# Token mixer of a 256-token block: gates as tanh, selection in two parts, norms ahead of splits

## The chip, the cores and the metric

The kernel is one program on one core of a Trainium2 chip. The metric is device time in microseconds (us) from launch to end, median of three runs. TensorE (PE) multiplies, ScalarE (ACT) and VectorE (DVE) work on rows of 128 partitions, GpSimd (POOL) and SyncE (SP) here issue the transfers from HBM.

## The reference, cut to what matters

Two transformer blocks follow each other on 256 tokens of width 1024. The change is in the token mixer of the second one:

```python
(qa, ka, va, qb, kb, vb, qi, ki, wi, xc, yc, gates) = split(xn @ w_in)
y_a = moba_attention(qa, ka, va, bias)                  # 8 heads, here plain causal
y_b = dsa_attention(qb, kb, vb, qi, ki, wi, bias)       # 8 heads, keys: the 64 best of
#   score = sum_h wi[h] * relu(qi[h] . ki), per query; others get -1e30
y_c = rg_lru(causal_depthwise_conv(xc, conv_w, conv_b), ...) * gelu(yc)
#   r, i = sigmoid(block matmuls); log_a = -8 r softplus(-lam); a = exp(log_a)
#   u = sqrt(1 - a*a) * i * x;  h[t] = a[t] h[t-1] + u[t]
g = sigmoid(gates).reshape(B, S, 3, 1024)
merged = g[:,:,0] * (y_a @ w_pa) + g[:,:,1] * (y_b @ w_pb) + g[:,:,2] * (y_c @ w_pc)
x = x + merged @ w_o
```

All is fp32. Each product is made from three matmuls: every operand is split into a high part (rounded to the matmul's input type) and a low part (the rest), and high x high, high x low and low x high are summed in PSUM.

## The kernel before, in words

Weights stream through four slots ("units" 0 to 3). For each step SP loads the four units of `raw`; ACT makes the high part `wh` (L1521), DVE the low part `wl` = `raw` - `wh` (L2243), and PE multiplies (L569 to L571). A unit of `wh` and `wl` is written again as soon as PE has used it, so that the two splits run one step ahead of PE: while PE is in a step, the units of the next are split one by one behind it. SP loads a unit again as soon as DVE has made its low part (`lo_done`).

The mixer's steps are, in order: qa, ka, va, xc, qi, kw, yc, qb, kb, vb, then g0 to g5 (the gates, 512 columns each), then pa, pb, pc (`step_down` and `rows_by_tile` on the three branches), then two halves of `w_o`. A gate step is 48 matmuls of 512 columns, 12 per unit. PSUM has two halves of four banks that the steps take in turn. When a step's sums are complete, ACT copies them out (`read_gate` L2031, `read_values`, `read_half`), DVE copies its share and tells PE that the half is free by a small memset on `emptied` (`close` L2276, `take_step` L3015). Side work of the attention uses the other half in the middle of a step: PE yields after each unit, waits for `emptied` of the step before (`other_emptied` L1290) and runs, for group n of four heads (n = 0, 1: branch a; 2, 3: branch b), `attend_scores(n)` (L1330), later `turn_probabilities(n)` (L1340 to L1342) and `attend_values(n)` (L1362). Between them DVE adds the bias (`biased(n)` L2948, L2950), and the maxima (`maxima(n)` L2962 to L2967, which for branch b also adds the selection's mask), ACT takes the exponents and their sums (`softmax(n)` L2045), DVE scales by the sums (`normalise(n)` L2974 to L2976), and both copy the turned probabilities out (`take_turned(n)` L2051 and L2981). `choose` (L2928) finds the 64 best by four rounds of `pick`, twice: a round is a maximum and a replacement of eight values for each of two tiles; the mask is written at the end. `convolve` (L3003) is the depthwise convolution, 12 instructions; its result is needed by the recurrent gates (`recurrent_gates` L1312, in step g3) and, since it shares memory with them, by gates g2 to g5.

The order of the work on each engine is written out by hand: ACT's list is the run of calls from L2080 on, DVE's from L3025 on, where `parts(u)` is the split of unit u. An engine's queue is strictly in order. PE's points are the ones in L1364 to L1490. After g5, DVE runs the recurrence (`tensor_tensor_scan` L3128), the product with gelu (L3131, `yc_ready`), low part (`yc_lo` L3134); ACT makes its high part (L2175); then DVE multiplies the gates into pa and pb (`gate_rows` L3141), adds, multiplies pc's tiles (`gate_tile` L3146), and adds them (`merge_tile` L3153, `merged`). PE turns the merged tiles (`turn_merged`, matmul line L1467), ACT and DVE make high and low parts (L2074, L3159), and the two `w_o` steps run on them.

ACT's functions live in tables; the compiler puts an `ACT_TABLE_LOAD` ahead of a function that is not in the table that is loaded.

Of the kernel before, what the change touches and what calls it, by code (L numbers as in the profile page):

```python
# [183 lines left out]
def build(nc, a, out):  # L184
    ctx = ExitStack()
    with ctx:
# [369 lines left out]
        def _(pe):  # L556
# [929 lines left out]
            for t, j in rows_by_tile(half, ctx_h, ctx_l, 0, True, False, wo_rows):  # L1486
                if (t, j) == (0, 1):
                    turn_merged(1, 4 - half)
                elif (t, j) == (0, 3):
                    pe.wait_ge(mg_lo, 2)  # L1490
# [14 lines left out]
        def _(act):  # L1505
# [525 lines left out]
            def read_gate(c):  # L2031

                hb = step_full()
                if c == 2:
                    act.wait_ge(xcv_ready, 1)
                T.mark(act.activation(gates3[c // 2][:, :, c % 2, :], ps[:, hb:hb + 2, :], ACT.Sigmoid), act_evac)
# [34 lines left out]
            def take_merged(t, half):  # L2071

                act.wait_ge(mg_turned, t + 1)
                T.mark(act.activation(uh[:, :, SEQ + t * P:SEQ + (t + 1) * P],  # L2074
                                      ps[:, half + 2 * t:half + 2 * t + 2, :].rearrange("p b (x n) -> p (b x) n", x=4), ACT.Copy), mg_hi)
# [60 lines left out]
            parts(0, 1, 2)  # L2136
            softmax(2, True)
            read_gate(0)
            softmax(2, False)
            parts(3)  # L2140
            parts(0, 1, 2)
            softmax(3, True)
            take_turned(2, even)
            read_gate(1)
            softmax(3, False)
            parts(3)
            parts(0)
            take_values(2, odd + 3)
# [24 lines left out]
            parts(3)  # L2173
            act.wait_ge(yc_ready, 1)
            T.mark(act.activation(uh[:, 0:4, SEQ:TOK], gy, ACT.Copy), yc_hi)  # L2175
            split()
# [55 lines left out]
        def _(vec):  # L2232
# [695 lines left out]
            def choose(last):  # L2928

                T.settle()  # L2930
                pick(TOPK // 16)
# [71 lines left out]
            def convolve():  # L3003
# [3 lines left out]
                for d in (1, 2, 3):  # L3007
# [51 lines left out]
            take_turned(1, odd)  # L3059
            parts(2)  # L3060
            take_values(1, odd + 3)
            take_step()
# [8 lines left out]
            choose(False)  # L3071
# [4 lines left out]
            choose(True)  # L3076
            parts(2)
            read_values(vab[:, 3, :])
            parts(3)
            parts(0)  # L3080
            biased(2, odd)
            maxima(2)
            parts(1, 2)
# [3 lines left out]
            biased(3, even)  # L3087
            parts(1)
            normalise(2)
            maxima(3)  # L3090
            parts(2)
            take_turned(2, even)
            take_step()
            parts(3)
            parts(0)
            take_values(2, odd + 3)
            normalise(3)
            parts(1)
            convolve()
            parts(2)  # L3100
# [26 lines left out]
            for m in range(4):  # L3127
                T.mark(vec.tensor_tensor_scan(out=xcv[:, m, :], data0=la[:, m, :], data1=it[:, m, :], initial=0.0,  # L3128
                                              op0=ALU.mult, op1=ALU.add), vec_own)
            T.settle()  # L3130
            T.mark(vec.tensor_tensor(gy, gy, xcv, ALU.mult), yc_ready)  # L3131
            parts(0, 1)
            vec.wait_ge(yc_hi, 1)
            T.mark(vec.tensor_tensor(ul[:, 0:4, SEQ:TOK], gy, uh[:, 0:4, SEQ:TOK], ALU.subtract), yc_lo)  # L3134
            parts(2, 3)

            def gate_rows(b):

                hb = step_full()
                o = (mg, mt)[b]  # L3140
                T.mark(vec.tensor_tensor(o, ps[:, hb:hb + 4, :], gates3[b].rearrange("p t c n -> p (t c) n"), ALU.mult), emptied)  # L3141

            def gate_tile(t, half):

                o = slice(2 * t, 2 * t + 2)
                T.mark(vec.tensor_tensor(mt[:, o, :], ps[:, half + 2 * t:half + 2 * t + 2, :], gates3[2][:, t, :, :], ALU.mult),  # L3146
                       emptied if t else vec_own)
# [7 lines left out]
            def take_merged(t, half):  # L3155
# [3 lines left out]
                T.mark(vec.tensor_tensor(ul[:, :, cols], ps[:, half + 2 * t:half + 2 * t + 2, :].rearrange("p b (x n) -> p (b x) n", x=4),  # L3159
                                         uh[:, :, cols], ALU.subtract), mg_lo)  # L3160

            gate_rows(0)
            split()
            gate_rows(1)
            T.settle()
# [203 lines left out]
```

## Time and profile before

| what | value |
|---|---|
| three runs | 1897.29, 1898.78, 1900.3 us; median 1898.78 |
| profiled execution | 1900.46 us, of which the span of its instructions is 1898.7 |
| PE, DVE, ACT busy | 95%, 60%, 44% of the span |
| the chain that ended last | PE 83%, DVE 8%, ACT 5%, DMA 2% |
| mixer | from 1407 to 1694 us of the span |
| a split on ACT (L1521), on DVE (L2243) | 1.02 and 1.18 us mean over the whole span |

PE is the engine that sets the time; what another engine costs is seen as idle time of PE, and in the clock that PE is granted. A table of waits names for each idle time the instruction that ended it.

### The profile page before, as it was taken

What the parts mean: (1) busy time and instruction counts of PE and PEld (TensorE: products, weight loads), DVE (VectorE), ACT (ScalarE), POOL (GpSimd) and SP (SyncE); (2) the same over time, 40 slices, a digit from 0 to 9 for tenths busy, and PEclk for the clock granted to TensorE, in tenths of its full rate; (3) what the DMA queues carried; (4) which work ended last, traced back from release to release, by engine and by line L of the source; (5) the groups of instructions that cost most, each with busy time, mean ns of one, the idle gap of its engine ahead of it and who ended that gap; (6) DMA issues with size and microseconds to landing.
All of it is one profiled execution on the core that took longest, in us unless ns stands there. A gap on an engine that the chain in (4) does not pass through costs nothing.

```text
span 1898.7 us, 26235 instructions
## 1 busy us (share of the span) xinstructions
PE 1804.6 (95%) x9865; PEld 1505.9 (79%) x9865; DVE 1142.8 (60%) x1523; ACT 841.9 (44%) x1211; POOL 86.9 (5%) x164
## 2 busy tenths in 40 slices
PE   5999999999999999999989998899989988989997
PEld 3877767778688888888878886899889966779986
DVE  2766757666367688544356554666655674765554
ACT  3334243342456423233255554565555545554453
POOL 3000101101000111000000000000010000000000
PEclk8999999999999999999999998899999998999999
DMA  8644544545265466333213221455554443545662
GB/s 294 197 150 132 171 149 148 158 130 171 73 242 177 142 212 187 117 86 111 99 43 129 85 90 55 155 178 177 199 166 152 155 146 100 186 135 177 182 194 100
DMA packets 150910, 282.38 MB, mean 149 GB/s; under 512 B 12652, under 2 KB 78308, under 8 KB 150689
## 3 DMA queue, kind: packets, MB, share of 16 engines
q1 hardware_dynamic: 133344, 220.54, 36.3%
q0 software_dynamic: 17472, 60.57, 10.3%
q8 instruction: 63, 1.03, 0.2%
q14 instruction: 31, 0.25, 0.0%
HBM read 276.83 MB, written 4.23 MB: 148 GB/s over the span
## 4 chain that ended last, share of the span: by engine, by line
PE 83%; DVE 8%; ACT 5%; DMA 2%; issue 2%; POOL 0%; SPq 0%; ACTq 0%; DVEq 0%; POOLq 0%
PE ps L569 24%; PE ps L570 23%; PE ps L571 23%; PE ps L841 4%; DVE wl L2243 2%; PE ps L834 1%; ACT wh L1521 1%; DMA arena<-in_norm_g 1%; PE ps L705 1%; PE ps L1126 1%; DMA raw<-in_ada_w 1%; PE ps L1107 1%; PE ps L783 1%; PE ps L718 0%; PE ps L614 0%
## 5 line engine op out<-in xcount | busy, mean ns | idle before, releaser
L2243 DVE TENSOR_TENSOR wl<-raw,wh 128x1024 fp32r<-128x1024 f32 (+1 forms) x388 | 454.4, 1181 | 394.0 <-ACT wh L1521 391.2
L1521 ACT ACTIVATE wh<-raw 128x1024 fp32r<-128x1024 f32 (+1 forms) x388 | 393.0, 1022 | 620.9 <-PE ps L571 600.8
L569 PE MATMUL ps<-uh,wh 128*128 128x256 f32 (+1 forms) x1216 | 381.7, 314 | 7.3 <-DVE spare L2265 7.3
L569 PE MATMUL ps<-wh,uh 128*128 128x512 f32 (+2 forms) x960 | 369.2, 385 | 13.2 <-issue 8.9
L570 PE MATMUL ps<-ul,wh 128*128 128x256 f32 (+1 forms) x1216 | 379.8, 312 | 0.0
L571 PE MATMUL ps<-uh,wl 128*128 128x256 f32 (+1 forms) x1216 | 379.5, 312 | 0.0
L570 PE MATMUL ps<-wl,uh 128*128 128x512 f32 (+2 forms) x960 | 355.8, 371 | 0.0
L571 PE MATMUL ps<-wh,ul 128*128 128x512 f32 (+2 forms) x960 | 355.2, 370 | 0.0
L569 PEld LDWEIGHTS ps<-uh,wh 128*128 128x128 f32 x1216 | 233.5, 192 | 22.4 <-issue 7.0
L571 PEld LDWEIGHTS ps<-uh,wl 128*128 128x128 f32 x1216 | 233.6, 192 | 12.6
L570 PEld LDWEIGHTS ps<-ul,wh 128*128 128x128 f32 x1216 | 233.5, 192 | 12.4
L569 PE MATMUL ps<-wh,ah 128*128 128x512 f32 x584 | 230.6, 395 | 4.9 <-DVE wl L2243 2.2
L569 PEld LDWEIGHTS ps<-wh,uh 128*128 128x128 f32 x960 | 183.3, 191 | 56.9 <-issue 25.9
L570 PE MATMUL ps<-wl,ah 128*128 128x512 f32 x584 | 228.3, 391 | 0.0
L571 PE MATMUL ps<-wh,al 128*128 128x512 f32 x584 | 228.2, 391 | 0.0
L570 PEld LDWEIGHTS ps<-wl,uh 128*128 128x128 f32 x960 | 183.3, 191 | 33.7 <-issue 5.3
L571 PEld LDWEIGHTS ps<-wh,ul 128*128 128x128 f32 x960 | 183.1, 191 | 31.1
L2304 DVE SCALAR_TENSOR_TENSOR arena<-arena,cvec 128x1024 f32<-128x1024 f32 x140 | 173.7, 1282 | 8.4 <-DVE res L2540 0.5
L569 PEld LDWEIGHTS ps<-wh,ah 128*128 128x128 f32 x584 | 110.3, 189 | 31.0 <-issue 7.3
L571 PEld LDWEIGHTS ps<-wh,al 128*128 128x128 f32 x584 | 110.2, 189 | 23.3
L570 PEld LDWEIGHTS ps<-wl,ah 128*128 128x128 f32 x584 | 110.4, 189 | 22.8 <-issue 0.5
L841 PE MATMUL ps<-res,arena 128*128 128x512 f32 x160 | 72.5, 600 | 3.0 <-DVE res L2540 2.1
(301 smaller groups left out, 1500.8 us busy)
## 6 DMA issues: line engine op xcount, KB each, us to landing
raw<-in_ffn_w_up SPq DMA_DIRECT2D x176, 256.0 KB
arena<-in_ada_w POOLq DMA_DIRECT2D x80, 512.0 KB, 4.1
raw<-in_w_in SPq DMA_DIRECT2D x60, 512.0 KB
raw<-in_ret_w_in SPq DMA_DIRECT2D x48, 512.0 KB
raw<-in_ffn_w_down SPq DMA_DIRECT2D x40, 512.0 KB
raw<-in_ret_w_out SPq DMA_DIRECT2D x32, 512.0 KB
raw<-in_w_up SPq DMA_DIRECT2D x32, 512.0 KB
raw<-in_w_down SPq DMA_DIRECT2D x32, 512.0 KB
```

Of the source, the lines that this page charges most:

```text
L569: pe.matmul(o, lh, rh, start=first, stop=False)
L570: pe.matmul(o, lh, rl, start=False, stop=False)
L571: return pe.matmul(o, ll, rh, start=False, stop=last)
L705: pe.matmul(o, ident[:, :], ident[:, :], start=True, stop=True)
L783: mm = pe.matmul(ps[32 * x:32 * x + 32, half + 3, 0:256], select[:, c, :], sums[q][:, c, x * 256:(x + 1) * 256], start=c == 0, stop=c == 1)
L834: mm = pe.matmul(o, qkt[:, 2 + f, k * P:(k + 1) * P], qkt[:, f, 0:n], start=f == 0, stop=f == 1)
L841: mm = pe.matmul(ps[:, half + t % 2, :], v0[:, c:c + P], vres[:, k, :], start=n == 0, stop=n == len(reads[t]) - 1)
L1107: mm = pe.matmul(ps[:, b + c, :], dqt[r, h, t * P:(t + 1) * P], dkt[r, h, :], start=True, stop=True)
L1126: mm = pe.matmul(ps[:, heads_v + h, t * P:(t + 1) * P], dpt[:, h, k, t * P:(t + 1) * P], dvs[i % 2][:, k, h * P:(h + 1) * P], start=k == 0 ...
L1521: T.mark(act.activation(wh[:, j, 0:size], raw[:, j, 0:size], ACT.Copy), hi_done)
L2243: T.mark(vec.tensor_tensor(wl[:, j, 0:size], raw[:, j, 0:size], wh[:, j, 0:size], ALU.subtract), lo_done)
L2304: ins = vec.scalar_tensor_tensor(out=o, in0=w, scalar=c32[:, k, c:c + 1], in1=o, op0=ALU.mult, op1=ALU.add)
```

## The change

The branch gates are held as tanh(x/2) where they were sigmoid(x); since sigmoid(x) = (1 + tanh(x/2)) / 2, the multiplications by a gate become (gate + 1) * sums in one instruction, and the factor 1/2 goes into the two places where the turned merged tile is read. On ACT and DVE the order is rewritten around g0 to g3 and around the recurrence, `convolve` is run in the step yc instead of g2, `choose` takes its number of rounds and is called with 4, 2 and 2 rounds, and PE turns the second merged tile one unit earlier. The full difference:

```diff
@@ -1484,7 +1484,7 @@
             G.next()
             pe.wait_ge(mg_lo, 1)
             for t, j in rows_by_tile(half, ctx_h, ctx_l, 0, True, False, wo_rows):
-                if (t, j) == (0, 1):
+                if (t, j) == (0, 0):
                     turn_merged(1, 4 - half)
                 elif (t, j) == (0, 3):
                     pe.wait_ge(mg_lo, 2)
@@ -2033,7 +2033,7 @@
                 hb = step_full()
                 if c == 2:
                     act.wait_ge(xcv_ready, 1)
-                T.mark(act.activation(gates3[c // 2][:, :, c % 2, :], ps[:, hb:hb + 2, :], ACT.Sigmoid), act_evac)
+                T.mark(act.activation(gates3[c // 2][:, :, c % 2, :], ps[:, hb:hb + 2, :], ACT.Tanh, scale=0.5), act_evac)
 
             def softmax(n, wide):
 
@@ -2072,7 +2072,7 @@
 
                 act.wait_ge(mg_turned, t + 1)
                 T.mark(act.activation(uh[:, :, SEQ + t * P:SEQ + (t + 1) * P],
-                                      ps[:, half + 2 * t:half + 2 * t + 2, :].rearrange("p b (x n) -> p (b x) n", x=4), ACT.Copy), mg_hi)
+                                      ps[:, half + 2 * t:half + 2 * t + 2, :].rearrange("p b (x n) -> p (b x) n", x=4), ACT.Copy, scale=0.5), mg_hi)
 
             def parts(*order):
 
@@ -2134,17 +2134,18 @@
             read_values(vab[:, 2, :])
             parts(3)
             parts(0, 1, 2)
+            read_gate(0)
+            parts(3)
+            parts(0)
             softmax(2, True)
-            read_gate(0)
             softmax(2, False)
-            parts(3)
-            parts(0, 1, 2)
-            softmax(3, True)
+            parts(1, 2)
             take_turned(2, even)
             read_gate(1)
-            softmax(3, False)
             parts(3)
             parts(0)
+            softmax(3, True)
+            softmax(3, False)
             take_values(2, odd + 3)
             parts(1, 2)
             take_turned(3, odd)
@@ -2171,9 +2172,10 @@
             parts(1, 2)
             read_gate(5)
             parts(3)
+            parts(0, 1)
             act.wait_ge(yc_ready, 1)
             T.mark(act.activation(uh[:, 0:4, SEQ:TOK], gy, ACT.Copy), yc_hi)
-            split()
+            parts(2, 3)
             split()
             S.base += 3
             par.base += 2
@@ -2925,10 +2927,10 @@
                                                  in_values=wk[:, t, 0:n], imm_value=MARK), vec_own)
                     T.settle()
 
-            def choose(last):
+            def choose(rounds, last=False):
 
                 T.settle()
-                pick(TOPK // 16)
+                pick(rounds)
                 if last:
                     for t, w in ((1, SEQ), (0, P)):
                         T.mark(vec.tensor_scalar(maskb[:, t, 0:w], wk[:, t, 0:w], MARK / 2, NEG, ALU.is_gt, ALU.mult), vec_own)
@@ -3000,11 +3002,11 @@
                 own(vec.scalar_tensor_tensor(out=wk[:, t, 0:n], in0=wk[:, t, 0:n], scalar=float(8 * HD) ** -0.5,
                                              in1=causal[:, t, 0:n], op0=ALU.mult, op1=ALU.add))
 
-            def convolve():
+            def convolve(*taps):
 
 
                 vec.wait_ge(xc_lin, 1)
-                for d in (1, 2, 3):
+                for d in taps:
                     T.settle()
                     for m in range(4):
                         c = CW0 + 4 * (3 - d) + m
@@ -3057,8 +3059,10 @@
             normalise(1)
             parts(1)
             take_turned(1, odd)
+            convolve(1)
             parts(2)
             take_values(1, odd + 3)
+            convolve(2, 3)
             take_step()
             parts(3)
             parts(0, 1)
@@ -3068,36 +3072,35 @@
             read_half(qkt5[:, 2])
             parts(3)
             parts(0, 1)
-            choose(False)
+            choose(TOPK // 16)
             parts(2)
             read_half(qkt5[:, 3])
             parts(3)
             parts(0, 1)
-            choose(True)
-            parts(2)
+            choose(TOPK // 32)
             read_values(vab[:, 3, :])
-            parts(3)
+            parts(2, 3)
+            choose(TOPK // 16 - TOPK // 32, True)
             parts(0)
             biased(2, odd)
+            parts(1)
             maxima(2)
-            parts(1, 2)
+            parts(2)
             take_step()
             parts(3)
             parts(0)
             biased(3, even)
+            normalise(2)
             parts(1)
-            normalise(2)
             maxima(3)
+            take_turned(2, even)
             parts(2)
-            take_turned(2, even)
             take_step()
             parts(3)
             parts(0)
+            normalise(3)
             take_values(2, odd + 3)
-            normalise(3)
-            parts(1)
-            convolve()
-            parts(2)
+            parts(1, 2)
             take_turned(3, odd)
             take_step()
             parts(3)
@@ -3125,26 +3128,29 @@
             T.settle()
             own(vec.tensor_tensor(it, it, lt, ALU.mult))
             for m in range(4):
+                if m == 2:
+                    parts(0)
                 T.mark(vec.tensor_tensor_scan(out=xcv[:, m, :], data0=la[:, m, :], data1=it[:, m, :], initial=0.0,
                                               op0=ALU.mult, op1=ALU.add), vec_own)
             T.settle()
             T.mark(vec.tensor_tensor(gy, gy, xcv, ALU.mult), yc_ready)
-            parts(0, 1)
+            parts(1)
             vec.wait_ge(yc_hi, 1)
             T.mark(vec.tensor_tensor(ul[:, 0:4, SEQ:TOK], gy, uh[:, 0:4, SEQ:TOK], ALU.subtract), yc_lo)
-            parts(2, 3)
+            parts(2)
 
             def gate_rows(b):
 
                 hb = step_full()
                 o = (mg, mt)[b]
-                T.mark(vec.tensor_tensor(o, ps[:, hb:hb + 4, :], gates3[b].rearrange("p t c n -> p (t c) n"), ALU.mult), emptied)
+                T.mark(vec.scalar_tensor_tensor(out=o, in0=gates3[b].rearrange("p t c n -> p (t c) n"), scalar=1.0, in1=ps[:, hb:hb + 4, :],
+                                                op0=ALU.add, op1=ALU.mult), emptied)
 
             def gate_tile(t, half):
 
                 o = slice(2 * t, 2 * t + 2)
-                T.mark(vec.tensor_tensor(mt[:, o, :], ps[:, half + 2 * t:half + 2 * t + 2, :], gates3[2][:, t, :, :], ALU.mult),
-                       emptied if t else vec_own)
+                T.mark(vec.scalar_tensor_tensor(out=mt[:, o, :], in0=gates3[2][:, t, :, :], scalar=1.0, in1=ps[:, half + 2 * t:half + 2 * t + 2, :],
+                                                op0=ALU.add, op1=ALU.mult), emptied if t else vec_own)
 
             def merge_tile(t):
 
@@ -3156,12 +3162,14 @@
 
                 vec.wait_ge(mg_hi, t + 1)
                 cols = slice(SEQ + t * P, SEQ + (t + 1) * P)
-                T.mark(vec.tensor_tensor(ul[:, :, cols], ps[:, half + 2 * t:half + 2 * t + 2, :].rearrange("p b (x n) -> p (b x) n", x=4),
-                                         uh[:, :, cols], ALU.subtract), mg_lo)
+                T.mark(vec.scalar_tensor_tensor(out=ul[:, :, cols], in0=ps[:, half + 2 * t:half + 2 * t + 2, :].rearrange("p b (x n) -> p (b x) n", x=4),
+                                                scalar=0.5, in1=uh[:, :, cols], op0=ALU.mult, op1=ALU.subtract), mg_lo)
 
             gate_rows(0)
-            split()
+            parts(3)
+            parts(0, 1, 2)
             gate_rows(1)
+            parts(3)
             T.settle()
             T.mark(vec.tensor_tensor(mg, mg, mt, ALU.add), vec_own)
             half = 4 * (par.base % 2)
```

On ACT, this is the stretch from vb's copy to the softmax of group 3 (`L2029` is vb's copy, `L2036` a gate's, `L2045` a softmax, `L2051` `take_turned`, `L2056` `take_values`). Before:

```order
L2029 ACTIVATE res<-ps 128x512
L1521 ACTIVATE wh<-raw 128x1024 x4
L2045 ACT_TABLE_LOAD
L2045 ACTIVATE arena,st<-arena,st 128x256 x4
L2036 ACT_TABLE_LOAD
L2036 ACTIVATE arena<-ps 128x2x512
L2045 ACT_TABLE_LOAD
L2045 ACTIVATE arena,st<-arena,st 128x128 x4
L1521 ACTIVATE wh<-raw 128x1024 x4
L2045 ACTIVATE arena,st<-arena,st 128x256 x4
L2051 ACTIVATE arena<-ps 128x1024
L2036 ACT_TABLE_LOAD
```

and in the changed kernel:

```order
L2029 ACTIVATE res<-ps 128x512
L1521 ACTIVATE wh<-raw 128x1024 x4
L2036 ACTIVATE arena<-ps 128x2x512
L1521 ACTIVATE wh<-raw 128x1024 x2
L2045 ACT_TABLE_LOAD
L2045 ACTIVATE arena,st<-arena,st 128x256 x4
L2045 ACTIVATE arena,st<-arena,st 128x128 x4
L1521 ACTIVATE wh<-raw 128x1024 x2
L2051 ACTIVATE arena<-ps 128x1024
L2036 ACTIVATE arena<-ps 128x2x512
L1521 ACTIVATE wh<-raw 128x1024 x2
L2045 ACTIVATE arena,st<-arena,st 128x256 x4
```

The gate's copy comes first, no table is loaded around a gate, and both halves of a softmax stand together, behind two splits.

On DVE, this is the end of the selection (`MAX` and `MATCH_REPLACE` are one round with their second tile, `L2914` or `L2916` vb's copy, the `MEMSET` behind it frees vb's PSUM half). Before:

```order
L2921 MAX st<-arena 128x8
L2924 MATCH_REPLACE arena<-st,arena 128x256 [waits vec_own]
L2924 MATCH_REPLACE arena<-st,arena 128x128
L2934 TENSOR_SCALAR arena<-arena 128x256 [waits vec_own]
L2934 TENSOR_SCALAR arena<-arena 128x128
L2243 TENSOR_TENSOR wl<-raw,wh 128x1024 [waits hi_done]
L2914 COPY res<-ps 128x512 [waits unit_used,lo_done]
L2265 MEMSET spare 1x1 [waits vec_own,act_evac]
L2243 TENSOR_TENSOR wl<-raw,wh 128x1024 [waits hi_done] x2
L2948 SCALAR_TENSOR_TENSOR arena<-ps,arena 128x1024 [waits z_loaded0,mix_scored]
```

and in the changed kernel, after four rounds in an earlier call and two here:

```order
L2926 MATCH_REPLACE arena<-st,arena 128x256 [waits vec_own]
L2926 MATCH_REPLACE arena<-st,arena 128x128
L2916 COPY res<-ps 128x512 [waits unit_used,vec_own]
L2267 MEMSET spare 1x1 [waits vec_own,act_evac]
L2245 TENSOR_TENSOR wl<-raw,wh 128x1024 [waits hi_done] x2
L2923 MAX st<-arena 128x8 [waits lo_done]
L2923 MAX st<-arena 128x8
L2926 MATCH_REPLACE arena<-st,arena 128x256 [waits vec_own]
L2926 MATCH_REPLACE arena<-st,arena 128x128
```

The copy and the memset now stand ahead of the last two rounds.

On PE, this is the one move, in the first `w_o` step (`L1467` turns merged tile 1):

```order
-L569 MATMUL ps<-wh,uh 128x512
-L570 MATMUL ps<-wl,uh 128x512
-L571 MATMUL ps<-wh,ul 128x512
-L569 MATMUL ps<-wh,uh 128x512
-L570 MATMUL ps<-wl,uh 128x512
-L571 MATMUL ps<-wh,ul 128x512
 L1467 MATMUL ps<-ident,arena 128x128 x8
```

Six matmuls stood ahead of the turn and now stand behind it.

## Rows read from the trace of the kernel before

**Rows 1.** Table of waits, PE, 1532 to 1604: total, times, longest us

```profile
PE ps L1330 <- DVE spare L2265: 5.4, 2, 3.6
PE ps L1340 <- DVE arena L2976: 4.9, 2, 3.8
PE ps L569 <- issue: 3.8, 1, 3.8
PE ps L569 <- ACT arena L2051: 0.8, 1, 0.8
```

**Rows 2.** Table of waits, PE, 1604 to 1694

```profile
PE ps L1467 <- DVE arena L3153: 3.2, 2, 1.7
PE ps L569 <- DVE wl L2243: 2.2, 1, 2.2
```

**Rows 3.** Stretches: busy PE, PEld, DVE, ACT, POOL, then PE clock, DMA share, GB/s

```profile
1532.00:1543.00 11.00, 7.41 (x31) 5.67 (x30) 9.93 (x21) 1.06 (x1) 0.00 (x0) 0.69 0.49 152
...
1560.00:1570.00 10.00, 6.15 (x27) 4.81 (x25) 9.60 (x13) 3.01 (x9) 0.00 (x0) 0.83 0.46 147
1586.00:1597.00 11.00, 7.18 (x27) 4.83 (x27) 5.55 (x11) 4.29 (x4) 0.00 (x0) 0.69 0.34 109
...
1604.00:1642.00 38.00, 38.00 (x168) 31.11 (x167) 21.61 (x26) 24.43 (x29) 0.00 (x0) 1.00 0.48 152
...
1664.00:1677.00 13.00, 9.76 (x51) 7.86 (x50) 10.62 (x10) 5.31 (x6) 0.00 (x0) 1.00 0.44 132
```

**Rows 4.** Timeline, DVE, end of the selection: start, length, what

```profile
1530.98 0.62 DVE L2921 MAX8 st<-arena 128x8 f32<-128x256 f32 x2
...
1533.86 0.43 DVE L2934 TENSOR_SCALAR arena<-arena 128x256 f32<-128x256 f32 x2
...
1536.27 0.06 DVE L2265 MEMSET spare<- 1x1 f32 x1
```

**Rows 5.** Timeline, ACT, softmax of group 2 and gate g0

```profile
1547.32 1.28 ACT L2045 ACT_TABLE_LOAD   x1
1548.61 0.51 ACT L2045 ACTIVATE arena<-arena,st 128x256 f32<-128x256 f32 x1
...
1552.00 1.02 ACT L2036 ACTIVATE arena<-ps 128x1024 f32<-128x1024 f32 x1
```

**Rows 6.** Timeline, DVE, step yc, then attention of groups 2 and 3

```profile
1495.35 0.06 DVE L2265 MEMSET spare<- 1x1 f32 x1 [4.13 <-ACT arena L2122]
...
1541.33 1.23 DVE L2962 TENSOR_TENSOR arena<-arena 128x1024 f32<-128x1024 f32 x1
...
1583.49 5.07 DVE L3011 SCALAR_TENSOR_TENSOR arena<-arena,gcol 128x255 f32<-128x255 f32 x12
```

**Rows 7.** Timeline, PE, side work at full clock

```profile
1553.36 1.58 PE L1330 MATMUL ps<-arena 64*128 64x256 f32 x16 [1.77 <-DVE spare L2265]
...
1600.46 3.67 PE L1319 MATMUL ps<-arena,rows 64*64 64x256 f32 x32
```

**Rows 8.** Timeline, DVE, recurrence and merge

```profile
1637.83 2.44 DVE L3128 TENSOR_TENSOR_SCAN arena<-arena 128x256 f32<-128x256 f32 x4
...
1643.61 2.36 DVE L2243 TENSOR_TENSOR wl<-raw,wh 128x1024 fp32r<-128x1024 f32 x2 [2.07 <-ACT wh L1521]
...
1658.56 2.29 DVE L3141 TENSOR_TENSOR arena<-ps,arena 128x2048 f32<-128x2048 f32 x1
...
1663.21 1.22 DVE L3146 TENSOR_TENSOR arena<-ps,arena 128x1024 f32<-128x1024 f32 x1
...
1672.78 1.22 DVE L3153 TENSOR_TENSOR arena<-arena 128x1024 f32<-128x1024 f32 x1
```

**Rows 9.** Timeline, ACT, first unit of pc

```profile
1649.87 1.06 ACT L1521 ACTIVATE wh<-raw 128x1024 fp32r<-128x1024 f32 x1 [3.45 <-DMA raw<-in_w_pc]
```

**Rows 10.** Table of waits, PE, 1110 to 1212

```profile
PE ps L1107 <- ACT arena L1937: 2.3, 1, 2.3
```

**Rows 11.** Stretch of that wait, columns as in rows 3

```profile
1146.00:1154.00 8.00, 5.67 (x20) 3.35 (x19) 5.88 (x11) 4.84 (x10) 0.00 (x0) 0.79 0.20 66
```

## Prediction

> **What bounds the kernel now.** I read the page first: PE is busy 95% of the span and makes 83% of the chain that ended last, so a change of order can only pay where PE waits, or where its clock is low. Then the table of waits of PE over the changed stretch, in two parts. From 1532 to 1604 (steps g0 to the recurrent gates in g3) PE waits 14.9 us in seven waits, three of them 3.6 to 3.8 us long [rows 1]. From 1604 to 1694 it waits 5.4 us [rows 2]. Then the stretches, for the clock: around each of the three long waits the granted clock is below 1: 0.69 over 11 us is 0.31 x 11 / 0.5 = 6.8 us at 1.2 GHz instead of 2.4, 0.83 over 10 us is 3.4 us, 0.69 over 11 us again 6.8 us [rows 3]; over 1664 to 1677, with two waits of at most 1.7 us, it stays at 1.00 [rows 3]. A 2.3 us wait elsewhere also stands in a stretch with 0.79 [rows 10, 11]. So a long wait is paid nearly twice. Last the timelines of DVE and ACT, for what each wait hangs on.
>
> PE's own work in the first part, at full clock: 168 matmuls of 512 columns take 38.0 us, 0.226 each [rows 3], so a unit (12) is 2.7 us and a step 10.9. From the end of g0's unit 0 (1532.8, where the first wait begins: 1536.4 less 3.6) to the end of the recurrent gates (1600.46 + 3.67 = 1604.1 [rows 7]) there are 13 units (35.3 us), two score groups of 1.5 [rows 7], two turns of 1.25 and two value groups of 1.45 (my estimates between a half and the whole of a score group, which has as many matmuls and more columns), and 3.6 of gates: 47.3 us. Before took 71.3. The 24.0 between are the 14.9 of waits, some 8 of half clock and small waits.
>
> **The change, part by part, first stretch.** I lay the new queues out from 1532.8. A split on DVE is 1.18 behind another (2.36 for two [rows 8]), on ACT 1.06 [rows 9].
>
> Wait 1 (3.6 us, the memset at 1536.27 that frees vb's PSUM half [rows 1, 4]). Four rounds end at 1533.86, where the mask begins; the third begins at 1530.98 [rows 4], so a round is 1.44. With two rounds now behind the copy, the copy starts at 1531.0, ends 1531.7, memset at 1531.8: ahead of 1532.8. Wait 1 goes. The rest moves behind: two splits to 1534.2, two rounds and mask to 1537.4, split (g1 unit 0) to 1538.6, bias 1.9 to 1540.5. PE leaves g0 at 1532.8 + 1.5 + 8.15 = 1542.5, so nobody waits for those.
>
> Wait 2 (1.8 us, memset behind gate g0's copy [rows 1]). Before, ACT reached the gate between the two parts of softmax(2), with table loads of 1.28 on both sides [rows 5]. Now the gate's copy is first: 1542.6 to 1543.6, without a load. But DVE must pass a split (1541.7), maxima(2) with mask (3.7: 1.23 for the first 1024 columns [rows 6], then 512, and the same for the reduction) to 1545.4, and a split, to 1546.6. PE needs the half at 1542.5 + 2.7 = 1545.2: a wait of 1.5 stays.
>
> Wait 3 (3.8 us, normalise(2) [rows 1]). PE: scores(3) to 1548.2, two units to 1553.7. ACT: split, split (needs g1 unit 0 used, 1545.2) to 1546.4, table load to 1547.6, eight exponents of group 2: four of 0.50 and four of 0.39, 3.6 in all, to 1551.3. DVE: two splits to 1549.1, bias(3) to 1551.0, normalise (0.2, 1.15 for 1024 columns as in a split, 0.7 for 512) from 1551.3 to 1553.5. Wait 3 goes, with 0.2 us to spare. The turn and a unit end at 1557.8.
>
> Wait 4 (0.8 us, ACT's copy of turned probabilities [rows 1]). ACT has no second softmax ahead of it any more. DVE does split, maxima(3) 3.6, copy: 1559.0. A wait of 1.2 instead of 0.8.
>
> Waits 5 and 6 (1.1 and 3.8 us; normalise(3), and the "issue" one [rows 1], which ends with DVE's copy behind the convolution's 5.07 [rows 6]). g2 starts at 1559.0; units and values(2) to 1568.6. ACT: gate g1 to 1558.9, two splits to 1562.8, softmax(3) without a load to 1566.4. DVE: normalise(3) to 1568.5: 0.1 to spare. Then take_values and two splits to 1571.5, copy 1572.2; PE needs it at 1568.6 + 1.3 + 2.7 = 1572.6. Both go. The convolution costs nothing where it now stands, in step yc: the last eight of its twelve instructions (3.4 us) stand where DVE waits 4.1 us for ACT [rows 6], the first four (1.7) in a wait of 3.3 shortly before. If that cover were gone it would cost up to 5.07.
>
> g3 then runs to the recurrent gates: 1572.6 + 2.7 + 1.5 + 2.7 + 3.6 = 1583.1. New total 50.3 us = 47.3 + 1.5 + 1.2 and 0.3 of rounding. Saved: 71.3 - 50.3 = **21.0 us**. The new sigmoid table load (ahead of the recurrent gates) lies beside their 3.6 us.
>
> A rule here bears on the margin of wait 3. The row has 1.28 for a load, and the exponent starts at 1548.61, 0.01 behind its end [rows 5]. The Trainium skill, "ScalarE: Activation LUTs", section "What ACT_TABLE_LOAD costs", adds a drain of about 1.38 us to the same load, 2.66 in all. By that the end of softmax(2) would slip by 1.38 and the saving would be some 19.8 (rival E); by the row it is 21.0, and the sum goes by the row.
>
> **Costs of the new operations.** Tanh from PSUM with a scale is not in the trace; between 1.02 (sigmoid, same shape [rows 5]) and 1.06 (a split [rows 9]); I take 1.02. The multiplication by (gate + 1) on 2048 columns was 2.29 as a plain product [rows 8]; the fused form takes 0.42 per 255 columns in series (5.07 / 12 [rows 6], 3.4 for 2048), and a plain 1024 takes 1.22 [rows 8]. I take 2.29, as the fused bias costs what the plain sum does in the 1.9 above; the upper end adds 1.1 on the chain once per gate_rows.
>
> **Second stretch** (in before's clock, 21.0 earlier in truth). PE ends pa at 1642.6. Before, DVE split pb's unit 0 only behind scans, product and ACT's high part, at 1643.61 [rows 8], wait 2.2 [rows 2]. Now ACT has split units 0 and 1 of pb before it waits for the product, and DVE splits unit 0 between scans (2.44 for four [rows 8]): 1639.0 to 1640.2. Scans and product end 1642.6, unit 1 at 1643.8, yc_lo 1644.9, unit 2 1646.0, gate_rows(0) 1648.3, unit 3 1649.5; PE needs them at 1645.3, 1648.0, 1650.7. The wait goes. pb ends 1653.5. pc's loads follow the low parts; before, unit 0 arrived 5 us behind its own (1649.87 [rows 9]); now at 1645.2, and unit 3 at 1654.5, split by 1657.4, needed 1657.6. DVE's chain from pb's end: 2.3 (gate_rows) + 1.2 (split) + 2.3 (sum) + 1.2 + 1.2: merged tile 0 at 1662.2, where before it was at 1665.8 (the split of pc's unit 3 stood ahead, but all started 3.6 later: 1658.56 [rows 8]). PE gets there at 1661.6: 0.6 instead of 1.6. From tile 0 to tile 1 the queues are as before, 8.2 us (1664.5 + 1.3 to 1672.78 + 1.2 [rows 8]): tile 1 at 1670.4.
>
> The turn of tile 1 now stands one unit (six matmuls, 1.36 us) earlier, PE reaches it at 1667.2 and waits **3.2 us**, where before it waited 1.7. What follows the turn is longer by those six, so the end gains 3.6 - 1.36 = 2.2 us, less the clock: three waits of 3.6 to 3.8 each came with 3.4 to 6.8 us at half clock [rows 1, 3], and so I charge 2.3 (half of some 4.6 us that lies outside the wait). The second stretch gives 0.
>
> Sum against the profiled execution: its time is 1900.46 (span 1898.7 and 1.8 around it), so 1900.5 - 21.0 + 0 = 1879.5. It stands 1.7 above the median of the three runs, 1898.78; against that, **1878 us**, own range 1876 to 1881.
>
> **Rivals.**
> A. The margins of 0.1 to 0.4 us don't hold. For: normalise(2) and (3), and the copy behind, stand at PE's very step, and every exponent read, semaphore and load in my layout is one I could have missed by 0.2. If softmax(2) and (3) come 1.5 to 2 us later, PE waits about 2.3 us twice and gets half clock both times (another 2 each, as in rows 10 and 11): 8.5 lost, 1886.5. Against: the queues are laid out in measured lengths.
> B. No half clock in the tail. For: a wait of 2.2 at 1645 [rows 2] had none. Against: 3.2 is nearer to 3.6. 1878 - 2.3 = 1875.5.
> C. Slower. The weights come late. ACT's softmax(2) now stands behind the split of g2's unit 0, whose load starts only when DVE has done g1's (1538.6, later than the units' own turn, as two rounds stand ahead), and DVE's normalise(2) stands in front of splits, maxima and frees. One transfer is late in this trace, 3.45 us [rows 9]. If g1, g2 and g3 each lost 7 us so, the 21 would be gone; at 8 us each, 1902. Against: 5 us from low part to loaded unit, and 6 to 7 between these points in my layout. It needs 12 us or more per load.
> D. Without effect: the waits are pushed on to the next semaphore, since DVE has the same work (only its order differs; it is busy 9.9 of 11 us [rows 3]). For: wait 2 and 4 partly stay. Against: from 1586 to 1597 it is busy only 5.6 of 11 us [rows 3], so there is room to push into. 1897.
> E. ACT needs time around a table load that I don't count, say as much again as the load, 1.28 [rows 5]: softmax(2) is late once, by 1.3 less 0.2 of margin, 1879.1. Against: the exponent at 1548.61 starts on the load's end [rows 5]. That there is such a drain is what the Trainium skill, "ScalarE: Activation LUTs" ("What ACT_TABLE_LOAD costs"), has.
>
> **How the numbers follow.** Forecast 0.69, A 0.12, B 0.11, C 0.03, D 0.02, E 0.03. The bounds: if every wait of rows 1 and 2 and all half clock went, 71.3 - 47.3 + 5.4 = 29.4 less, 1869.4, which needs waits that I see stay. Lower end 1873 (B with all rounding in its favour); the upper end takes in A: 1887. This leaves out C, D, and the edges, under 0.15. A measurement here tells 0.2%, 3.8 us, from no change: faster 0.95, same 0.02, slower 0.03.
>
> **What would show it.** In the profile after: ACT's table loads between g0 and g5 are five fewer, PE's waits for the memset at g0 and for L2976's successor (normalise) are gone or under 0.5 us, one wait of some 1.5 us stays at scores(3) and one of 1.2 before g2, the first stretch's clock is 1.00, pb starts without a wait, and PE's longest wait in the mixer is the one at the second turn, some 3 us, with half clock behind it. The prediction is wrong if normalise(2) or (3) is waited for over 1 us, if the transfer of a unit is waited for in g1 to g3, or if waits of the same size appear in g3 to g5.

## The result, and the profile after

The changed kernel takes 1878.14 us (median of four, 1877.09 to 1881.74) against 1898.4 of the kernel before on the same chip: a ratio of 0.9888, 95% interval 0.9876 to 0.99, so 20.3 us less. The profiled execution took 1877.86 us, its span is 1876.1.

To compare stages I take the start of the first score group (L1330, 1444.3 in before, 1442.6 after) as zero: the 1.7 us between those two come from code that the change doesn't touch, and this start varies from 1441.7 to 1447.0 over all runs below. From it, in us, read off the PE timeline of each run (one profiled execution each; a mark is the start of the instruction named):

| run | scores(2) starts | last matmul of the recurrent gates | first turn | second turn | first norm matmul |
|---|---|---|---|---|---|
| before | 92.1 | 159.5 | 221.6 | 229.8 | 250.2 |
| changed | 88.4 | 139.4 | 197.7 | 205.9 | 229.3 |
| changed, again | 88.5 | 139.4 | 197.7 | 205.9 | 229.4 |

So 20.1 us were gained up to the recurrent gates and 3.8 more up to the first turn, and 3.0 were lost behind the second: 20.9 in the mixer. The table of waits of PE in the changed kernel (engine, line, who ended the wait: total, times, longest us), first from g0 to the recurrent gates, then to the end of the mixer:

```profile
PE ps L569 <- issue: 1.1, 1, 1.1
PE ps L1330 <- DVE spare L2267: 1.0, 1, 1.0
```

```profile
PE ps L1467 <- DVE arena L3159: 3.4, 2, 3.0
```

Of the six waits of [rows 1] the table has two left, 2.1 us instead of 14.9; of [rows 2] the one ahead of pb is gone, the first turn waits 0.4, the second 3.0 instead of 1.7. The stretches (columns as in [rows 3]) show the clock:

```profile
1524.00:1582.00 58.00, 55.78 (x308) 43.59 (x306) 44.77 (x73) 32.86 (x59) 0.00 (x0) 1.00 0.55 168
...
1646.00:1654.00 8.00, 5.52 (x22) 4.59 (x23) 4.81 (x6) 1.02 (x1) 0.00 (x0) 0.79 0.66 195
```

The whole first stretch has the full clock, where [rows 3] had three spells of half clock; behind the second turn there is now one, 0.21 x 8 / 0.5 = 3.4 us. PE is busy through it (behind the turn the matmuls start 0.43 us apart instead of 0.23).

DVE at the end of the selection, to be held against [rows 4]:

```profile
1528.90 0.69 DVE L2916 COPY res<-ps 128x512 f32<-128x512 f32 x1
1529.72 0.06 DVE L2267 MEMSET spare<- 1x1 f32 x1
1529.73 2.36 DVE L2245 TENSOR_TENSOR wl<-raw,wh 128x1024 fp32r<-128x1024 f32 x2
1532.12 0.62 DVE L2923 MAX8 st<-arena 128x8 f32<-128x256 f32 x2
```

The memset is out ahead of g0's first unit, and the last two rounds follow while PE multiplies. ACT around gate g0 and softmax(2), against [rows 5]:

```profile
1541.05 1.03 ACT L2036 ACTIVATE arena<-ps 128x1024 f32<-128x1024 f32 x1 [1.66 <-PE ps L571]
1541.98 1.05 ACT L1521 ACTIVATE wh<-raw 128x1024 fp32r<-128x1024 f32 x1
1543.77 1.06 ACT L1521 ACTIVATE wh<-raw 128x1024 fp32r<-128x1024 f32 x1 [0.75 <-PE ps L571]
1544.85 1.28 ACT L2045 ACT_TABLE_LOAD   x1
1546.14 0.51 ACT L2045 ACTIVATE arena<-arena,st 128x256 f32<-128x256 f32 x1
```

The gate's tanh has no load ahead of it, and one load is left for the exponents, with the next instruction 0.01 us behind its end. DVE's normalise(2), the instruction that TensorE waited 3.8 us for in [rows 1]:

```profile
1549.79 0.20 DVE L2976 RECIPROCAL st<-st 128x8 f32<-128x8 f32 x1 [1.02 <-ACT arena L2045]
1550.03 1.23 DVE L2977 TENSOR_TENSOR arena<-arena,st 128x1024 f32<-128x1024 f32 x1
1551.17 0.68 DVE L2978 TENSOR_TENSOR arena<-arena,st 128x512 f32<-128x512 f32 x1
```

It ends at 1551.85, and PE turns group 2 at 1552.0. The table of waits has none there, but PE could have started 0.25 us earlier: where the probabilities lie ready, as in e9 below, the first matmul of the turn starts 0.23 behind that of the last one of the unit, here 0.48. First the changed kernel, then e9:

```profile
1551.52 0.39 PE L571 MATMUL ps<-wh,ul 128*128 128x512 f32 x1
1552.00 0.30 PE L1340 MATMUL ps<-ident,arena 128*128 128x128 f32 x1
```

```profile
1551.78 0.39 PE L571 MATMUL ps<-wh,ul 128*128 128x512 f32 x1
1552.01 0.27 PE L1340 MATMUL ps<-ident,arena 128*128 128x128 f32 x1
```

The convolution in step yc, against the wait of 4.13 us in [rows 6]:

```profile
1484.46 1.67 DVE L3013 SCALAR_TENSOR_TENSOR arena<-arena,gcol 128x255 f32<-128x255 f32 x4
...
1489.60 3.36 DVE L3013 SCALAR_TENSOR_TENSOR arena<-arena,gcol 128x254 f32<-128x254 f32 x8
1493.63 0.06 DVE L2267 MEMSET spare<- 1x1 f32 x1 [0.66 <-ACT arena L2122]
```

DVE still waits for ACT behind it, 0.66 us. The recurrence, against [rows 8]:

```profile
1615.95 1.27 DVE L3133 TENSOR_TENSOR_SCAN arena<-arena 128x256 f32<-128x256 f32 x2
1617.15 1.20 DVE L2245 TENSOR_TENSOR wl<-raw,wh 128x1024 fp32r<-128x1024 f32 x1
...
1631.85 2.29 DVE L3146 SCALAR_TENSOR_TENSOR arena<-arena,ps 128x2048 f32<-128x2048 f32 x1 [0.41 <-PE ps L571]
```

pb's first unit is split between the scans. The fused multiplication takes 2.29 us, what the plain one took, and DVE now waits for PE ahead of it.

### The profile page after: what moved, and what is told of

Read it like the earlier page. It is cut to its first block and busy times, and to the rows that moved or that the text cites. A ratio compares the mean times of both kernels' runs of the same rounds, so it can differ in the third digit from the quotient of the medians.

```text
span 1876.1 us, 26231 instructions
## 1 busy us (share of the span) xinstructions
PE 1797.3 (96%) x9865; PEld 1501.4 (80%) x9865; DVE 1142.5 (61%) x1523; ACT 836.0 (45%) x1206; POOL 87.0 (5%) x164
## 3 DMA queue, kind: packets, MB, share of 16 engines
q8 instruction: 63, 1.03, 0.2%
```

## Experiments

Theory: the gain comes from what stands ahead of what in two queues, in four parts that can be undone one by one (selection, convolution, order around the softmax, recurrence), tanh is a small part, and the earlier turn costs time. Rivals: the table loads are the gain; or the waits are only pushed about. The same marks for all kernels, with medians and the ratio to before (95% interval):

| run | scores(2) | gates end | first turn | second turn | norm | median us | ratio |
|---|---|---|---|---|---|---|---|
| e1 sigmoid | 88.4 | 141.2 | 199.6 | 207.8 | 229.6 | 1882.54 | 0.9917 (0.9899 to 0.9935) |
| e2 selection late | 91.7 | 145.4 | 203.7 | 211.9 | 233.7 | 1881.76 | 0.9912 (0.9895 to 0.9929) |
| e3 convolution late | 88.5 | 146.4 | 204.7 | 212.9 | 236.4 | 1882.63 | 0.9912 (0.9896 to 0.9929) |
| e7 old order | 88.5 | 146.5 | 204.8 | 213.0 | 236.5 | 1884.46 | 0.9922 (0.9905 to 0.9938) |
| e4 turn later | 88.5 | 139.4 | 197.7 | 206.0 | 226.4 | 1874.81 | 0.9869 (0.9852 to 0.9885) |
| e5 tanh alone on before | 92.1 | 153.2 | 215.3 | 223.5 | 244.0 | 1895.35 | 0.9972 (0.9962 to 0.9982) |
| e6 recurrence undone | 88.5 | 139.4 | 201.4 | 209.6 | 233.1 | 1882.01 | 0.9911 (0.9895 to 0.9928) |
| e8 four moves | 88.5 | 138.4 | 196.8 | 203.8 | 224.6 | 1875.74 | 0.987 (0.9853 to 0.9886) |
| e9 softmax first | 88.5 | 137.1 | 195.4 | 202.5 | 223.3 | 1871.7 | 0.9849 (0.9833 to 0.9866) |

The experiments ran on three chips; each ratio is to the kernel before on the same chip. The medians say the same as the marks in sign, not in size. Against the changed kernel's 1878.14 they are 4.4 us longer in e1, 3.6 in e2, 4.5 in e3 and 6.3 in e7, where the norm marks are 0.3, 4.4, 7.1 and 7.2 later. The profiled execution was the shortest of four in e1 (1878.87 of up to 1885.31) and the longest in e3 (1887.37, the others 1882.21 to 1882.81). So each size below is that of one profiled execution, read by its marks. How far they repeat is known for the parts that an edit leaves alone: the gates end at 139.4 in the changed kernel, its repeat, e4 and e6.

**e1, the gates as sigmoid.** In the changed kernel:

```diff
-...ps[:, hb:hb + 2, :], ACT.Tanh, scale=0.5), act_evac)
+...ps[:, hb:hb + 2, :], ACT.Sigmoid), act_evac)
# and the four (gate + 1) and 0.5 instructions as before
```

> The changed kernel with the gates as sigmoid again; all else as changed. My theory is that the gain of the first stretch (g0 to the recurrent gates) comes from what stands ahead of what, and that the table loads matter only where a margin is thin. Some five more loads of 1.28 us on ScalarE: the one behind gate g0 shifts softmax(2) by about 0.5 us (it had 0.75 us of waiting ahead of it), the two around gate g1 shift softmax(3) by 1.3, so TensorE waits about 0.3 more at the turn of group 2 and 1.2 at the turn of group 3; 1880 us, 1.5 to 2.5 over the changed kernel. Rival (the loads are the gain): 1886 or more, with waits of over 2 us before the turns and half clock behind them.

Measured: the gates end 1.8 us later. The norm mark is only 0.3 later, as this profile has no half clock behind the second turn; the median is 4.4 over the changed kernel's, more than the 1.5 to 2.5 expected. The table of waits of PE, g0 to g3:

```profile
PE ps L1340 <- DVE arena L2978: 1.6, 2, 1.1
PE ps L569 <- issue: 1.2, 1, 1.2
PE ps L1330 <- DVE spare L2267: 1.0, 1, 1.0
```

The 1.6 stands in two waits, 0.5 at the turn of group 2 (where the changed kernel is 0.25 late already) and 1.1 at that of group 3. ACT there:

```profile
1541.80 1.28 ACT L2036 ACT_TABLE_LOAD   x1 [1.64 <-PE ps L571]
1543.09 1.03 ACT L2036 ACTIVATE arena<-ps 128x1024 f32<-128x1024 f32 x1
...
1546.03 1.28 ACT L2045 ACT_TABLE_LOAD   x1
```

The load ahead of the gate is swallowed in part by the 0.75 us that the next split would have waited. By the marks the theory's size holds. That the loads are the gain does not: no wait is over 1.2 us and the median is 1882.54, where that rival had over 2 us and 1886 or more.

**e2, the selection in one piece.**

```diff
-            choose(TOPK // 32)
+            choose(TOPK // 16, True)
+            parts(2)
             read_values(vab[:, 3, :])
-            parts(2, 3)
-            choose(TOPK // 16 - TOPK // 32, True)
+            parts(3)
```

> The changed kernel with the last selection in one piece of four rounds again, ahead of vb's copy. Theory: the wait for vb's memset is back with 3.6 us and half clock behind it (2.7 us), and nothing behind absorbs it, since VectorE does the same work in all; bias(2) comes a little earlier than it would else, so part is won back at the wait before scores(3): 1883 to 1884.5, 5 to 6.5 over the changed kernel. Rival (the waits are only pushed about): within 1.5 us of the changed kernel.

Measured: 6.0 later at the gates' end. The first wait is back, with half clock:

```profile
PE ps L1330 <- DVE spare L2267: 3.2, 1, 3.2
PE ps L1340 <- DVE arena L2978: 1.2, 1, 1.2
PE ps L569 <- issue: 1.1, 1, 1.1
```

```profile
1528.00:1542.00 14.00, 10.81 (x45) 8.48 (x44) 9.39 (x23) 3.24 (x4) 0.00 (x0) 0.76 0.45 143
```

0.24 x 14 / 0.5 = 6.7 us at half clock, part of it inside the wait. From the marks and the spacing of the matmuls the first wait costs 3.2 and the clock 2.7. The expectation had something won back ahead of scores(3), and the wait of 1.0 there is gone, but one of 1.2 at the turn of group 2 stands in its place. The norm comes 4.4 later only, since half clock is absent behind the second turn.

**e3, the convolution in g2.** `convolve(1)` and `convolve(2, 3)` taken out of step yc, and

```diff
-            parts(1, 2)
+            parts(1)
+            convolve(1, 2, 3)
+            parts(2)
             take_turned(3, odd)
```

> The changed kernel with the convolution back in step g2, ahead of the last copy of turned probabilities. Theory: VectorE's copy comes 5.1 us later, TensorE had 0.4 to spare there and waits some 4 us, with half clock behind it (2 to 3 us): 1884, 5.5 to 7 over the changed kernel. Nothing changes in step yc, where VectorE waits longer for ScalarE. Rival (VectorE's idle time of 2.3 us behind that copy absorbs half of it): 1881.

Measured: 7.0 later. PE waits 4.3 us for DVE's copy ("issue", two waits with the one ahead of g2), and the clock around it is 0.77 over 15 us:

```profile
PE ps L569 <- issue: 5.3, 2, 4.3
PE ps L1330 <- DVE spare L2267: 1.4, 1, 1.4
```

```profile
1570.00:1585.00 15.00, 10.65 (x53) 8.08 (x51) 9.47 (x19) 5.11 (x5) 0.00 (x0) 0.77 0.36 106
```

From the turn of group 3 to values(3) PE takes 7.0 us more than in the changed kernel, 4.5 of waiting (counted from when the next matmul could have started) and 2.5 of clock. DVE's idle time behind the copy absorbed nothing, since PE waits for the copy itself: the rival falls. And without the convolution in step yc scores(2) starts at 88.5, as with it: it was free there.

**e7, the old order of softmax, gate, norms and splits** (both queues in g0 to g2 as in before; ACT's):

```diff
-            read_gate(0)
-            parts(3)
-            parts(0)
             softmax(2, True)
+            read_gate(0)
             softmax(2, False)
-            parts(1, 2)
...
```

> The changed kernel with the queues of ScalarE and VectorE in g0 to g2 in the order of before (softmax in two halves around the gate's copy, splits ahead of the norms), but with tanh, the selection in two parts and the early convolution kept. Theory: TensorE waits some 2 us before scores(3), 3 at the turn of group 2 and 2.8 before g2 (ScalarE's copy behind softmax(3)), the last two with half clock behind them: 1886 us, 7 to 9 over the changed kernel. Rival (tanh, selection and convolution are enough and the order on its own is worth little): within 2.5 us of the changed kernel.

Measured: 7.1 later, with these waits:

```profile
PE ps L569 <- ACT arena L2051: 2.4, 1, 2.4
PE ps L1330 <- DVE spare L2266: 1.9, 1, 1.9
PE ps L1340 <- DVE arena L2977: 1.8, 1, 1.8
```

By the marks the order is worth as much as the selection or the convolution. It is undone as a whole here, so which of its moves (softmax, norms or splits) does how much is not shown. The three waits are where they were expected, each smaller by 0.1 to 1.2 us, and the total is in the range. Half clock is not where it was expected: it stands behind the wait of 1.9 before scores(3) (0.83 from 1542 to 1552) and behind the one of 2.4 (0.83 from 1565 to 1575), and not behind the 1.8 at the turn of group 2 (1.00 from 1555 to 1565).

**e5, tanh alone on the kernel before** (the reverse of e1's edit, applied there).

> The kernel before with the gates as tanh and nothing else. Theory: there the table loads stand on the chain, one ahead of and one behind each of gates g0 and g1 inside a softmax: the wait before scores(3) goes from 1.8 to 0.5, the one at the turn of group 2 from 3.8 to 2.5, that of group 3 is gone, the one for VectorE's copy goes from 3.8 to 2.2; the first wait of 3.6 stays: 5 to 8 us less than before, 1892. So tanh is worth some 6 us in the old order and 1.8 (measured by undoing it) in the new one. Rival (the loads lie beside PE in the old order too): within 2 us of before.

Measured: 6.3 earlier at the gates' end and 5 us in the median, ratio 0.9972. PE's waits, against [rows 1]:

```profile
PE ps L1330 <- DVE spare L2265: 4.1, 2, 3.6
PE ps L569 <- issue: 2.7, 1, 2.7
PE ps L1340 <- DVE arena L2976: 2.4, 1, 2.4
PE ps L569 <- ACT arena L2051: 0.8, 1, 0.8
```

So the same edit is worth 6.3 in the old order, where a load stood on either side of each gate inside a softmax, and 1.8 in the new one. The four things undone one by one add to 1.8 + 6.0 + 7.0 + 7.1 = 21.9, against 20.1 for all together. That the sum comes near doesn't make the parts independent: tanh, with 6.3 in one order and 1.8 in the other, is not.

**e6, pb's splits behind the recurrence** (all split calls around the recurrence and `gate_rows`, on ACT and DVE, as in before).

> The changed kernel with the splits of pb's units behind the recurrence again, on both engines. Theory: the wait of 2.2 us ahead of pb is back and the one at the first turn grows from 0.4 to 1.6: the first turn comes 3.5 us later, nothing else changes, 1881.5. Rival (VectorE's chain from pb to merged tile 0 sets the turn alone, and the wait ahead of pb is absorbed in it): the first turn comes at most 1.5 us later.

Measured: the first turn 3.7 later. The two waits are back, the third is the 3.0 of the changed kernel:

```profile
PE ps L1467 <- DVE arena L3156: 4.6, 2, 3.0
PE ps L569 <- DVE wl L2244: 2.2, 1, 2.2
```

**e4, the turn one unit later.**

```diff
-                if (t, j) == (0, 0):
+                if (t, j) == (0, 1):
```

> The changed kernel with the second merged tile turned one unit later in the first w_o step, as before. Theory: that edit alone costs time: TensorE reaches the turn 1.36 us later, at the same arrival of the tile, so the wait is 1.7 instead of 3.0, the six matmuls lie ahead of it, and half clock is not seen behind a wait of 1.7. The first norm matmuls come 1.4 us earlier, 3 where the changed kernel had half clock there: 1876 us. Rival (the earlier turn pays, as it gives ScalarE and VectorE cover for the split of tile 1): 1878 or above, with a wait ahead of the second row of the w_o step.

Measured: the second turn starts at the same time (206.0), since the tile sets it; the wait is 1.7 instead of 3.0, and the norm matmuls come 3.0 us earlier:

```profile
PE ps L1467 <- DVE arena L3159: 2.0, 2, 1.7
```

So 1.4 is the six matmuls and 1.6 the clock, which is 1.00 here behind the turn. This part of the change costs time.

**e8, four moves**: e4's, and on DVE `take_step` ahead of `parts(2)` in g0, `take_turned(2)` ahead of `maxima(3)`, `merge_tile(1)` ahead of `parts(2)`.

> The changed kernel with four moves: the turn of tile 1 one unit later, VectorE frees gate g0's half ahead of the split of g1's unit 2, takes the turned probabilities of group 2 ahead of maxima(3), and adds merged tile 1 ahead of the split of w_o's unit 2. Theory: the waits of 1.0 before scores(3) and 1.1 before g2 go (softmax(3) has over 3 us of waiting ahead of it, so that later maxima cost nothing), 1.4 at the turn as in the other run, 0.9 more from the earlier tile: 4.4 us earlier at the end of the mixer, up to 6 with the clock: 1873. Rival (a move only brings the next wait: for unit 2's low part in g1, or for softmax(3)): 1876, no better than the later turn alone.

Measured: 4.7 earlier than the changed kernel at the norm, 1.8 earlier than e4, of which only 1.0 in the first stretch. The rival was half right: the waits of 1.0 before scores(3) and 1.1 before g2 are gone, but one of 1.2 at the turn of group 2 and one of 0.4 before values(2) have come in their place.

```profile
PE ps L1340 <- DVE arena L2978: 1.2, 1, 1.2
PE ps L1467 <- DVE arena L3159: 0.9, 2, 0.5
PE ps L1362 <- DVE spare L2267: 0.4, 1, 0.4
```

The median isn't below e4's; their spreads (1873.08 to 1878.57, 1874.47 to 1876.12) overlap, so the 1.8 us of the marks is not shown in the whole time.

**e9, softmax(2) ahead of the split that waits for PE**, on top of e8:

```diff
             read_gate(0)
             parts(3)
-            parts(0)
             softmax(2, True)
             softmax(2, False)
-            parts(1, 2)
+            parts(0, 1, 2)
```

and on DVE `biased(3)` and `normalise(2)` ahead of `parts(0)`.

> The kernel of e8 with softmax(2) directly behind gate g0's copy and one split on ScalarE, and on VectorE bias(3) and normalise(2) ahead of the split of g2's unit 0. In e8 the wait before scores(3) was gone and one of 1.2 us at the turn of group 2 stood in its place, since softmax(2) stands behind a split that waits for TensorE. Theory: softmax(2) ends 1.5 us or more earlier, that wait and the 0.35 before values(2) go, and the end of the mixer comes 1.5 us earlier than in e8, 6.2 earlier than in the changed kernel; 1873 to 1874 with the noise of 1 to 2 us that the rest of the kernel shows. Rival (something else is next, such as the split of g2's unit 0 or bias(3), which waits for the scores): no earlier than e8.

Measured: 1.3 earlier than e8 at the gates' end, 6.0 earlier than the changed kernel at the norm. ACT no longer waits for PE between the gate and the exponents (in e8 0.75 us ahead of the second split), and two waits of 0.4 are all that the table of PE has from g0 to the first turn:

```profile
PE ps L1362 <- DVE spare L2266: 0.4, 1, 0.4
PE ps L1467 <- DVE arena L3157: 0.4, 1, 0.4
```

It takes 1871.7 us (1870.91 to 1873.13) against 1878.48 of the changed kernel (1877.9 to 1881.02) and 1900.08 of the one before on the same chip.

**The changed kernel again.**

> The changed kernel once more, unchanged, beside the others on one chip. The intervals between the mixer's marks should repeat within 0.2 us. Open is whether half clock follows the 3.0 us wait at the second turn: with the same wait it came in three of five profiles (the changed kernel, e3, e7; not in e1, e2). Theory: it depends on when the wait falls, not on its length alone, so it may be absent here with the same wait; then the end of the mixer comes 1.7 us earlier than in the first profile. Rival: a wait of 3.0 decides it, and e1 and e2 differ in something else; then it is there again.

Measured: 1878.48 us, the marks repeat within 0.1, and half clock is there again at the same mark. The theory allowed that it might be absent in the same kernel, and it wasn't. But the wait's length doesn't decide it alone: e1 has the same wait at the second turn,

```profile
PE ps L1467 <- DVE arena L3158: 3.4, 2, 3.0
```

and full clock around it:

```profile
1646.00:1656.00 10.00, 6.98 (x36) 5.57 (x35) 7.40 (x8) 2.59 (x3) 0.00 (x0) 1.00 0.64 195
```

## Why the prediction was right

By its own steps:

- Waits 1, 3, 5 and 6 go, and an undone part brings each back: wait 1 in e2, 3 in e7, 5 in e1, 6 in e3. For wait 3 the prediction had 0.2 us to spare and the trace has none: normalise(2) ends 0.1 behind the moment when PE is ready, and the turn starts 0.25 late. At the turn of group 3, with 0.1 to spare by the prediction, it starts on time, 0.23 behind the last unit's matmul. So rival A's doubt of the margins was half right, but its waits of 2.3 us didn't come.
- Wait 2 stays at 1.5: measured 1.0. Wait 4 at 1.2: measured 1.1.
- First stretch 21.0: measured 20.1. The term that was mis-sized is PE's own work of 47.3 us, with every matmul of the units at 0.226 from start to start. In the changed kernel the first matmul behind a side group has 0.31 to 0.34 to the next one, and as much lies between the last one of a unit and values or the gates. That is 0.14 to 0.24 us in each of the six stretches of units from scores(2) to the recurrent gates, some 1.2 us in all; why the matmuls start later there is not shown. One such start, and the turn 0.25 late:

```profile
1544.67 1.58 PE L1330 MATMUL ps<-arena 64*128 64x256 f32 x16 [0.99 <-DVE spare L2267]
1546.18 0.50 PE L569 MATMUL ps<-wh,uh 128*128 128x512 f32 x1
1546.51 0.40 PE L570 MATMUL ps<-wl,uh 128*128 128x512 f32 x1
```

  From scores(3) to the turn that makes 7.3 (1552.0 - 1544.67), where the prediction had 1.5 + 5.4 = 6.9. It outweighs the 0.6 that the two waits came out shorter.
- The count of waits in the prediction is off: [rows 1] has six, not seven. Their sum of 14.9, on which the working rests, is right.
- Costs: the fused multiplication is 2.29 as taken and the tanh 1.02 to 1.03, taken as 1.02; the upper ends didn't come.
- Second stretch 0: measured 0.8 gained (250.2 - 159.5 against 229.3 - 139.4). The first turn waits 0.4, predicted 0.6; the second 3.0, predicted 3.2; half clock is there and costs 1.6, predicted 2.3. e4 confirms that the earlier turn costs 1.4 and the clock.
- That 1878 was hit within 0.2 us is luck in part: the gain of the first stretch came out 0.9 smaller than forecast and that of the second 0.8 larger, and the two cancel. The measured median itself is one of four from 1877.09 to 1881.74.
- Table loads: five fewer, and they are not what gave the time in the new order (e1). The exponent starts 0.01 us behind the load's end in the changed kernel too (1544.85 + 1.28, 1546.14), so rival E falls. The Trainium skill's further drain of 1.38 ("ScalarE: Activation LUTs", "What ACT_TABLE_LOAD costs") is not seen in these rows, and the measurement decides. No unit came late in g0 to g3, so C falls.
- D is refuted by e2, e3 and e7, which lose 6.0 to 7.1. In before DVE waited 4.7, 3.7, 3.8 and 3.7 us for ACT between 1548 and 1578, and the moved work has that room. D does hold for one wait: where the one before scores(3) goes (e2, e8), the turn of group 2 waits 1.2 in its place.

What stays open is why the same 3.0 us wait at the second turn has half clock behind it in five profiles and none in two (below).

## What to carry to other kernels

When two in-order queues feed a matmul engine that never rests, lay out all three in measured lengths from one mark, and ask of each instruction which wait it stands in front of: here nearly the same work in another order, with five table loads fewer, was worth 20 us, and a whole 5 us convolution was free in one step and cost 7 in another. A long wait has to be counted with the half clock behind it: 2.7 us on 3.2 in e2, 2.5 on 4.3 in e3. A margin of 0.2 us in such a layout is no margin, as the turn of group 2 shows. And a cost undone in the new arrangement (tanh 1.8) is not what it was worth in the old one (6.3): try both ends.

## What the runs showed of the hardware

Waits of 3.2 to 4.3 us of PE in the mixer (before, e2, e3, e5) all had half clock with them. Between 1.9 and 3.0 us it went either way: in e7 the waits of 1.9 and 2.4 had it, while the 2.2 ahead of pb in before and in e6, and one of 2.1 at 1406.7 us of the span of before, had not (clock 1.00).

Half clock behind the second turn's wait of 3.0 us came in the changed kernel, its repeat, e3, e6 and e7, where the wait began 202.9, 202.9, 209.9, 206.6 and 210.0 us after the mark, and not in e1 and e2, where it began at 204.8 and 208.9. From turn to norm it makes 23.4 to 23.5 against 21.8 us. So the length of the wait doesn't decide it alone; that it is the moment at which the wait falls is a guess, which no run tests by moving one wait and nothing else.
